# Low parts of the feed-forward weights: one 2048-column VectorE instruction for two chunks

## The reference

```python
y = _rms(h, norm_ffn_g[i])
h = h + (jax.nn.silu(y @ w_gate[i]) * (y @ w_up[i])) @ w_down[i]
y = _rms(h, norm_ple_g[i])
h = h + jax.nn.sigmoid(y @ w_ple_gate[i]) * (p[i] @ w_ple_proj[i])
```

## Time and profile before

| | us |
|---|---|
| median of 3 runs | 1418.76 (1418.65 to 1419.2) |
| span of the profiled execution | 1417.2 |
| time of the profiled execution | not listed apart; taken as the median, 1418.8 |
| TensorE busy | 1411.0 |
| VectorE busy | 893.2 |
| ScalarE busy | 714.8 |
| a weight load, from issue to landing (median by matrix) | 3.8 to 5.5 |

### The profile page before, as it was taken

The page is one execution under the profiler, slowest core; times in us unless marked ns, Lnnn a source line. Parts: engine busy times, 40 slices in busy tenths (PEclk is TensorE's granted clock), DMA queues, the critical chain, the costliest instruction groups (busy, mean ns, idle before and its releaser), DMA issues.

```text
span 1417.2 us, 17665 instructions
## 1 busy us (share of the span) xinstructions
PE 1411.0 (100%) x6365; PEld 1157.6 (82%) x6365; DVE 893.2 (63%) x1093; ACT 714.8 (50%) x981; POOL 78.6 (6%) x64
## 2 busy tenths in 40 slices
PE   9999999999999999999999999999999999999999
PEld 7888888888888888888888888888888887777887
DVE  6589976665545555455555445556767759896653
ACT  7477755554444433444434344345556647665442
POOL 2000010000000000000000000000000134330000
PEclk9999999999999999999999999999999999999999
DMA  9767657676776656677666667667768688889752
GB/s 331 250 204 218 199 182 251 221 253 193 225 222 224 221 195 195 193 222 221 216 199 227 192 192 222 195 223 237 254 224 279 208 274 250 255 274 298 251 195 89
DMA packets 171735, 318.07 MB, mean 224 GB/s; under 512 B 11954, under 2 KB 35758, under 8 KB 171545
## 3 DMA queue, kind: packets, MB, share of 16 engines
q1 hardware_dynamic: 156792, 285.37, 63.2%
q10 hardware_dynamic: 13088, 25.18, 5.7%
q0 software_dynamic: 1792, 6.71, 1.4%
HBM read 293.04 MB, written 24.17 MB: 224 GB/s over the span
## 4 chain that ended last, share of the span: by engine, by line
PE 97%; DVE 1%; DMA 1%; ACT 0%; POOL 0%; issue 0%; SPq 0%; ACTq 0%; DVEq 0%
PE acc L1566 31%; PE acc L1567 31%; PE acc L1568 31%; PE acc L1628 1%; PE sp L1779 1%; PE tp L1795 1%; DVE w_lo L1013 1%; PE tp L1586 0%; DMA wide<-parked 0%; DMA parked<-wide 0%; ACT w_hi L660 0%; DMA resid<-in_x 0%; POOL rs L596 0%; PE tp L1618 0%; PE sp L1706 0%
## 5 line engine op out<-in xcount | busy, mean ns | idle before, releaser
L1013 DVE TENSOR_TENSOR w_lo<-w_raw,w_hi 128x1024 fp32r<-128x1024 f32 x488 | 599.0, 1231 | 483.6 <-ACT w_hi L660 482.5
L660 ACT ACTIVATE w_hi<-w_raw 128x1024 fp32r<-128x1024 f32 x499 | 527.5, 1060 | 635.3 <-PE acc L1568 630.9
L1566 PE MATMUL acc<-w_lo,yh 128*128 128x512 f32 x1056 | 411.3, 389 | 0.0
L1568 PE MATMUL acc<-w_hi,yl 128*128 128x512 f32 x1056 | 410.8, 389 | 0.0
L1567 PE MATMUL acc<-w_hi,yh 128*128 128x512 f32 x1056 | 410.8, 389 | 0.0
L1566 PE MATMUL acc<-w_lo,hh 128*128 128x512 f32 x784 | 307.5, 392 | 0.0
L1568 PE MATMUL acc<-w_hi,hl 128*128 128x512 f32 x784 | 305.3, 389 | 0.0
L1567 PE MATMUL acc<-w_hi,hh 128*128 128x512 f32 x784 | 305.2, 389 | 0.0
L1566 PEld LDWEIGHTS acc<-w_lo,yh 128*128 128x128 f32 x1056 | 198.2, 188 | 42.0 <-issue 0.6
L1568 PEld LDWEIGHTS acc<-w_hi,yl 128*128 128x128 f32 x1056 | 198.2, 188 | 41.3
L1567 PEld LDWEIGHTS acc<-w_hi,yh 128*128 128x128 f32 x1056 | 198.2, 188 | 40.8
(11 more groups left out here) (172 smaller groups left out, 701.1 us busy)
## 6 DMA issues: line engine op xcount, KB each, us to landing
w_raw<-in_w_gate SPq DMA_DIRECT2D x88, 512.0 KB, 4.3
w_raw<-in_w_up SPq DMA_DIRECT2D x88, 512.0 KB, 4.4
w_raw<-in_w_down SPq DMA_DIRECT2D x88, 512.0 KB, 4.2
w_raw<-in_w_in SPq DMA_DIRECT2D x64, 512.0 KB, 4.6
w_raw<-in_swa_w_in ACTq DMA_DIRECT2D x48, 512.0 KB, 5.5
w_raw<-in_w_out SPq DMA_DIRECT2D x32, 512.0 KB, 4.4
w_raw<-in_w_ple_gate SPq DMA_DIRECT2D x32, 512.0 KB, 5.5
w_raw<-in_swa_w_out SPq DMA_DIRECT2D x32, 512.0 KB, 4.1
```

The lines of the kernel that those rows point to most:

```text
L660: act.activation(w_hi[:, s % SPL], w_raw[:, s % RAW], ACT.Copy).then_inc(hi_ready, 1)
L1013: dve.tensor_tensor(w_lo[:, s % SPL], w_raw[:, s % RAW], w_hi[:, s % SPL].bitcast(F32), ALU.subtract).then_inc(lo_ready, 1)
L1566: pe.matmul(dst, xh[:, f, tk], w_lo[:, s % SPL, k], start=(f == 0), stop=False)
L1568: last = pe.matmul(dst, xl[:, f, tk], w_hi[:, s % SPL, k], start=False, stop=(f == CK * n - 1))
```

## The change

`split_two` writes the low parts of two neighbouring chunks with one instruction of 2048 columns. It waits until the high parts of both are there and raises `lo_ready` by two. In the feed-forward block it is called at every odd chunk, and the even chunk has no call of its own. The other blocks keep the single form.

```diff
+            def split_two(s, lap=ONCE):
+
+                a, b = s % SPL, s % RAW
+                dve.wait_ge(hi_ready, s + 2 + 8 * lap.oct)
+                dve.tensor_tensor(w_lo[:, a:a + 2], w_raw[:, b:b + 2], w_hi[:, a:a + 2].bitcast(F32),
+                                  ALU.subtract).then_inc(lo_ready, 2)
+
...
             def pair(s, u, lap, before, n=None, kt=None, first=False):
                 for c in range(16):
-                    split(s + c, lap)
+                    if c % 2:
+                        split_two(s + c - 1, lap)
...
                 for n in range(len(DOWN)):
-                    split(START[FFN_UNIT + 8] + n, lap)
+                    if n % 2:
+                        split_two(START[FFN_UNIT + 8] + n - 1, lap)
...
             for n in range(len(TAIL)):
-                split(START[base + 4] + n)
+                if n % 2:
+                    split_two(START[base + 4] + n - 1)
```

## The result

| | before | changed |
|---|---|---|
| median of 7 runs each, us | 1419.04 (1418.58 to 1419.81) | 1422.97 (1422.0 to 1424.63) |
| ratio | | 1.0029, 95% interval [1.0018, 1.0039] |
| profiled execution: time, span, us | about 1418.8, 1417.2 | 1424.63, 1422.9 |

What follows compares the result with a forecast made beforehand. TensorE's stream was taken as the bound. Stalls of 0.4 + 2.5 + 0.2 = 3.1 us, plus 0.1 for thin covers, gave 3.2 us on 1418.8: 1422.0 us, 0.23% slower, range 1419.4 to 1426.0 us.

Steps and rivals of the forecast that it cites:

- TensorE's stream is the bound, VectorE's saving is worth nothing: Whole feed-forward block: TensorE almost never waits, so VectorE's 20 us of saving cannot shorten the run.
- Cost of the wide instruction: VectorE's 2048-column subtraction: 2.31 us, bounds 2.21 and 2.35; 132 wide ones take 305 us where 264 narrow took 325.
- Term 1: First lap, chunk 0: the first pair waits for the second high part, stalling TensorE once, 0.4 us.
- Term 2: Last down-projection: late put and reordered VectorE work make chunk 22 late, stalling TensorE 2.5 us; bounds 1.5 and 4.5.
- The low bound: Chunk 22, last down-projection: with a first trip of 3.83 us the squares decide, and the stall is 1.5 us.
- Term 3: Following block, chunk 4: the next put stands behind a load waiting for chunk 22's low part; stall 0.2 us.
- the formula g - 5.0: Following block, chunk 4: stall for a put-to-fetch trip of g us; 0.2 us for 5.2, none for 3.8, 1.1 for 6.1.
- Thin covers: Chunk 10 of the laps and other places costed at nothing, cover 0.2 to about 3 us; 0.1 us added.
- That rival: The laps stall as well: each of eight loses about 1 us at chunk 10, about 1430 us; chance 5%.
- The pause lowers the clock: Rival: after the pause TensorE's clock falls to 1.2 GHz, 3 to 6 us extra, about 1426 us; chance 3%.

Runs made afterwards that it cites:

- three pairs were apart: Changed kernel with chunks 0, 1 of each lap and 14, 15 and 22, 23 of the last down-projection single again: 1418.85 us, ratio 0.9998.
- the earlier put: Changed kernel with one call moved on SyncE's queue, so the first residual block's put precedes the load of chunk 22: 1420.96 us, ratio 1.0012.
- five, six and seven extra: Kernel before with 5, 6 or 7 extra VectorE subtractions ahead of chunk 12's low part in the gated-embedding block: 1419.9, 1422.41, 1423.69 us.
- the last down-projection alone: Changed kernel with the wide instruction kept only in the last down-projection, single low parts elsewhere: 1422.69 us, ratio 1.0026.
- chunk 22 apart: Changed kernel with chunks 22 and 23 of the last down-projection given single low parts in their old places: 1420.71 us, ratio 1.0012.

## Why the prediction was right, and where it was not

The forecast was 1422.0 us in a range of 1419.4 to 1426.0; 1422.97 was measured. Direction, place and mechanism of the stall were right; that the clock adds to it was held unlikely and happened in two of seven runs. By its steps:

- **TensorE's stream is the bound, VectorE's saving is worth nothing.** Shown: 18 us less on VectorE changed nothing once three pairs were apart.
- **Cost of the wide instruction, 2.31 us.** That was the line through two narrower shapes; 2.29 was measured.
- **Term 1, 0.4 us.** 0.42 in the trace, and 0.5 us in the times of the kernel without the wide last down-projection.
- **Term 2, 2.5 us.** 2.2 measured. With the 2.0 us taken off, each station lay within 0.3 us of the forecast: the puts at 982.8 and 992.2 (forecast 982.6 and 992.0), the second high part at 1001.4 (1001.5), the pair at 1005.3 (1005.35), TensorE's return at 1007.6 (1007.7). The trips took 5.17 and 5.10 us for the 5.2 and 4.96 taken. The low bound, with the squares and not the trip in charge, was 1.5 us; that case, made on the chip by the earlier put, came 1.5 us late. For what hangs on the put's place in the queue there is a rule: the Trainium skill (DMA: Bandwidth & Descriptors, "Queues, rings and completion order") lets a DMA engine take a queue's descriptors in ring order. Right behind one load the trip was 5.17 us, ahead of that load 3.93, and right behind six 9.6. That fits the rule, but a single load just ahead cost less than the 6.1 us that I had worked out by it, and no run tells the order in the queue from the mere sharing of the DMA engines. The trips also vary by themselves: in the kernel before and those with five, six and seven extra, which are the same up to there, the second took 4.93 to 5.61 us and the third 6.05 to 9.03. So that 5.2 and 4.96 came out so closely is in part luck.
- **Term 3, 0.2 us.** It showed in the kernel with the last down-projection alone, 0.48 us late. The trip there took 5.89 us, for which the formula g - 5.0 gives 0.9, so neither the trip nor the steps behind it were exact. With chunk 22 apart it grew to 0.76 us, because the six loads then bunch ahead of the put. The prediction didn't see that removing the stall of term 2 raises the stall of term 3.
- **Thin covers.** No lap shows a wait at chunk 10. That rival falls.
- **The pause lowers the clock, 3%.** This was the step that failed. The reasoning was that TensorE had stood still for 2.4 us in the first 36 with the clock at 1.00. That is a sum of four gaps: 1.64 us before the first matmul of all, and 0.35, 0.33 and 0.12 us between matmuls. It says nothing about one pause of 2.2 us. The gaps of 1.64 and 0.12 us moreover lie in the first 5.2 us, where TensorE ran at the lower pace anyway. Two of seven runs of the changed kernel had the fall, four of seven with the last down-projection alone. The Trainium skill (TensorE: Matmul & The Clock Gate, "Part 1: The HAM clock gate") says that the clock is halved after an idle pause and comes back after sustained work; the two traces with a fall agree, at 0.50 for 3.4 us and back at 1.00 while TensorE worked. Which pauses bring a fall, and how often, is known here from the counts in the table alone. The size was off as well: 1.4 and 1.6 us a fall in the two traces, not 3 to 6.

As measured the steps sum to 0.42 + 2.21 + 0.48 = 3.1 us, the third from the kernel with the last down-projection alone, and 0.3 us for the second matmul behind each pause, some 0.1 us late, which the prediction left out: 3.4 us. The five runs at full clock had a median 3.3 us above before. That the forecast's 3.2 came so close is in part luck: term 2 was 0.3 us too long and term 3 as much too short. The two runs with the fall lie 2.0 us above those five, more than the 1.4 to 1.6 us that a fall costs in the traces; only one of the two was traced, and 1.58 us of its time is the slow start. With both the median of all seven is 1422.97 us, without them 1422.37.

## What to carry to other kernels

Joining two instructions into one also joins when their results are there and when their inputs must be. Follow that through every queue that waits for the first result, loads and puts too, and not only to the consumer. Here a saving of 18 us on an engine off the bound bought nothing, and places where other work stands ahead of a joined pair can be left single. Where the sum gives TensorE a pause such as the 2 to 3 us here, add the price of a lower clock for the work behind it.

## What the runs showed of the hardware that I had not expected

- The fall came 1.0 us after TensorE had resumed from a 2.2 us pause in one trace, and 0.4 us before its return from a 3.4 us pause in another. It lasted 3.4 us both times.
- With the same program, whose one traced execution has a pause of 2.0 us, six of eleven runs had the fall and five had not.
- At the start of an execution TensorE ran at about half pace, until 5.2 us in the kernel before and until 10.5 us in the traced execution of the changed one, where the latter had lost 1.6 us by 36 us.
- A pause costs some 0.1 us beyond its length: the second matmul after it starts 0.34 us behind the first, not 0.23 (1009.62 and 1009.96).
- From a put to its fetch it took 5.1 to 5.2 us with a load issued 0.4 us ahead at the first trip, 3.8 to 3.9 us in the kernel before and with the put ahead of that load, and 9.6 us with six loads within 3.3 us ahead. With three pairs apart the first trip took 5.2 us although its load was 1.2 us ahead, as in the kernel before, so that distance alone does not decide. The second trip took 4.93 to 5.61 us in four programs that do not differ up to there.
